# Down projection of a fused two-block kernel: one order of the k pairs for both halves, and the sums of weight blocks on GpSimd instead of VectorE

## The chip, the cores and the metric

One Trainium2 chip, one of its cores. Times are device microseconds (us) of one execution; the profile's durations of single instructions are in nanoseconds (ns) where marked. TensorE multiplies, VectorE and ScalarE prepare its operands, GpSimd does very little in this kernel, and SyncE's queue issues nearly all loads.

## The reference, cut to what matters

Two transformer blocks on a sequence of 256 tokens with a model width of 2048, all in float32. The change lies in the last stage of the second block, the down projection of the feed-forward part and the final norm:

```python
h = rmsnorm(x, g_ffn[l])
u = causal_dwconv(h @ w_up[l], ffn_conv_w[l]) + ffn_conv_b[l]
gate, val = jnp.split(u, 2, axis=-1)
x = x + (jax.nn.silu(gate) * val) @ w_down[l]
...
return rmsnorm(x, g_final)
```

`w_down` has 5632 rows (44 tiles of 128, taken as 22 k pairs of two tiles) and 2048 columns (four chunks of 512).

## The kernel before, in words

**How a product is made.** A float32 weight is split into a rounded part (hi) and the rest (lo). ScalarE copies a unit of 128x1024 weights from its stage into hi (line 676, `round_down`), VectorE subtracts hi from the stage to get lo (line 683, `rest_down`), and TensorE multiplies in three passes, activation-hi by weight-hi, activation-hi by weight-lo and activation-lo by weight-hi (lines 1245 to 1247). TensorE waits for `lo_ready` of each unit; ScalarE may round unit j only when TensorE has used unit j - 6, since hi and lo are rings of six slots (`DOWN_RING`). In the feed-forward stage ahead of it the same work is done at lines 346 and 351, with rings of four.

**Units of the down projection.** There are 116 units (`down_units`, line 131). A *row unit* is one k pair in one chunk of 512 columns: 2 k tiles x 2 token tiles x 3 passes = 12 matmuls of 512 columns. Its weights come through a ring of four stages. K pairs 7 to 21 are done in this way. K pairs 0 to 6 are done for two chunks at once by seven block products in place of eight (Strassen's scheme in Winograd's form): four units, here called s0 to s3, and 7 x 3 = 21 matmuls. Each uses up 6, 3, 6 and 6 of them. Their weights come into `pair_stage`, which holds two pairs. s0 and s1 are blocks as loaded; s2 and s3 need four sums of blocks, each 128x512, made in place in `pair_stage` after lo of s1 is done: two sums, then a signal (`sums_ready`) for which ScalarE's rounding of s2 waits, then two more sums and a signal for which the rounding of s3 waits. Before the change VectorE makes them, inside `rest_down` (lines 688 to 692). The activations' sums for these pairs are made earlier, in the feed-forward loop.

**The order.** The 2048 columns are done in two halves (chunks 0 and 1, then 2 and 3). `DOWN_PAIRS` (line 127) gives each half's order: a list of k pairs becomes row units, first all for the lower chunk, then all for the upper one; a bare number is one seven-product pair. In the first half the last list is `[20, 21]`, so the last seven-product pair is followed by four row units; in the second half it is `[18, 19, 20, 21]`, followed by eight. Every engine runs through the 116 units in this order: at step j ScalarE and VectorE prepare unit j + 5 (`prepared_at`, line 158; a little differently for the first steps) and do what else is due:

- steps 0 to 2: the last convolution, gate and activation of the feed-forward loop (`ffn_sums`, `ffn_conv`, `ffn_act`), on VectorE between its rests of units 3, 4 and 5;
- one and two steps after the last seven-product pair of a half (`SEVEN_END`): `add_sevens`, eight sums on VectorE that put the seven products into x;
- at the last row unit of a chunk (`DOWN_END`): `add_to_x` (line 454), which frees the chunk's two accumulator banks. Two pairs of banks take turns, so the first row unit of chunk 2 waits for `add_to_x` of chunk 0;
- two steps later `apply_gain` (line 2126): x of the chunk times the final gain, two products of 128x512. It waits for the squares of the chunk (line 530, ScalarE).

SyncE's queue issues the loads in the order of lines 773 to 779. A row load waits until lo of the unit four row units earlier is done; a pair's load waits until lo of s3 of the pair before the last is done. The first two pair loads wait until TensorE has finished the feed-forward stage, as `pair_stage` shares memory with that stage's operands. GpSimd's queue ends with the load of the final gain (line 872), after the last activation.

At the end, the last four row units are multiplied for token tile 0 first and then for tile 1 (lines 1289 to 1301). VectorE then finishes each tile: the last sum (line 2177), a reciprocal square root of 12 small steps, and two scalings; ScalarE scales the first half of the row (line 1611) and SyncE stores.

Of the kernel before, what the change touches and what calls it, by code (L numbers as in the profile page):

```python
# [33 lines left out]
LAYERS = 2  # L34
# [89 lines left out]
OUT_PAIRS = [0, 1, 2, 6, 7, 3, 4, 5]  # L124

SEVEN = 7
DOWN_PAIRS = [[[7, 8], 0, [9, 10], 1, [11, 12], 2, [13, 14], 3, [15, 16], 4, [17, 18], 5, [19], 6, [20, 21]],
              [[7, 8], 0, [9, 10], 1, [11, 12], 2, [13, 14], 3, [15], 4, [16], 5, [17], 6, [18, 19, 20, 21]]]


def down_units():

    units = []
    for chunk, items in enumerate(DOWN_PAIRS):
        for item in items:
            if isinstance(item, list):
                units += [("rows", k, 2 * chunk + half) for half in range(2) for k in item]
            else:
                units += [(f"seven{part}", item, chunk) for part in range(4)]
    return units  # L140


DOWN = down_units()
U_DOWN = len(DOWN)
DOWN_END = [max(j for j, unit in enumerate(DOWN) if unit[0] == "rows" and unit[2] == c) for c in range(4)]
SEVEN_END = [max(j for j, unit in enumerate(DOWN) if unit[0] == "seven3" and unit[2] == chunk) for chunk in range(2)]
DOWN_TAIL = U_DOWN - 4
DOWN_ROWS = [j for j, unit in enumerate(DOWN) if unit[0] == "rows"]
SEVEN_FIRST = [j for j, unit in enumerate(DOWN) if unit[0] == "seven0"]
# [3 lines left out]
def sevens_until(j):  # L153

    return sum(first <= j for first in SEVEN_FIRST)


def prepared_at(u):

    ahead = {0: [3], 1: [4], 2: [5], 3: [6, 7], 4: [8, 9]}.get(u, [u + 5])  # L160
    return [j for j in ahead if j < U_DOWN]
# [40 lines left out]
def build(nc, dram, out):  # L202
# [12 lines left out]
    with ctx:  # L215
        def sb(name, shape, dt=F32, stack=ctx):
            return stack.enter_context(nc.sbuf_tensor("sb_" + name, shape, dt))

        def sem(name):
            return ctx.enter_context(nc.semaphore(name))  # L220
# [9 lines left out]
        pair_stage = sb("pair_stage", [P, 2, 2, UNIT], F32, down)  # L230
# [29 lines left out]
        lo_ready = sem("lo_ready")  # L260
# [11 lines left out]
        mix_loaded, gfin_loaded, stored = sem("mix_loaded"), sem("gfin_loaded"), sem("stored")  # L272
# [12 lines left out]
        roped, pool_step = sem("roped"), sem("pool_step")  # L285
# [19 lines left out]
        sums_ready, first_copied, seven_free = sem("sums_ready"), sem("first_copied"), sem("seven_free")  # L305
# [148 lines left out]
        def add_to_x(dve, base, j, pair, c):  # L454

            multiplied(dve, base, j)
            for t in range(T):
                cols = x[:, t, c * 512:(c + 1) * 512]
                ins = dve.tensor_tensor(cols, acc[:, 2 * pair + t, :], cols, ALU.add)
            ins.then_inc(acc_free[pair], 1)  # L460
# [163 lines left out]
        U4 = U3 + N_FFN * U_FFN  # L624
# [23 lines left out]
        def down_parts(j):  # L648

            kind = DOWN[j][0]  # L650
            hi, lo = down_slot(j)
            if kind == "rows":
                return stage[:, DOWN_ROWS.index(j) % RING, :], hi, lo
            pair = pair_stage[:, (sevens_until(j) - 1) % 2, :, :]
            by_part = lambda ap: ap.rearrange("p (k n) -> p k n", n=512)
            if kind == "seven0":
                return pair[:, 0, :], hi, lo
            if kind == "seven1":
                return pair[:, 1, 512:UNIT], hi[:, 0:512], lo[:, 0:512]
            return pair[:, :, 0:512] if kind == "seven2" else pair[:, :, 512:UNIT], by_part(hi), by_part(lo)  # L660
# [14 lines left out]
            src, hi, _ = down_parts(j)  # L675
            act.activation(hi, src, ACT.Copy).then_inc(hi_ready, 1)

        def rest_down(step, dve, j):


            dve.wait_ge(hi_ready, U4 + (j + 1))
            src, hi, lo = down_parts(j)
            dve.tensor_tensor(lo, src, hi.bitcast(F32), ALU.subtract).then_inc(lo_ready, 1)
            if DOWN[j][0] == "seven1":
                pair = pair_stage[:, (sevens_until(j) - 1) % 2, :, :]
                b11, b22, b12, b21 = pair[:, 0, 0:512], pair[:, 0, 512:UNIT], pair[:, 1, 0:512], pair[:, 1, 512:UNIT]
                dve.wait_ge(lo_ready, U4 + (j + 1))
                step(dve.tensor_tensor(b11, b11, b12, ALU.add))
                dve.tensor_tensor(b12, b12, b22, ALU.add).then_inc(sums_ready, 1)
                dve.wait_ge(sums_ready, 2 * sevens_until(j) - 1)  # L690
                step(dve.tensor_tensor(b22, b11, b22, ALU.add))
                dve.tensor_tensor(b21, b22, b21, ALU.add).then_inc(sums_ready, 1)

        with nc.Block() as block:

# [93 lines left out]
            def _(pool):  # L789
# [29 lines left out]
                with pool.Fori(0, LAYERS) as layer:  # L819

                    pairs = layer * (C_LAYER // 2) + C_MEM // 2
                    step = Steps(pool, pool_step, layer * 19)
# [47 lines left out]

                pool.wait_ge(act_ready, N_FFN)
                pool.dma_start(gfin[:, :], dram["g_final_2"].partition_broadcast(P)).then_inc(gfin_loaded, 16)


            @block.tensor
# [740 lines left out]
            def _(dve):  # L1616
                step = Steps(dve, dve_step)
# [83 lines left out]
                with dve.Fori(0, LAYERS) as layer:  # L1701
# [6 lines left out]
                    step = Steps(dve, dve_step, layer * DVE_STEPS_LAYER + steps_before)  # L1708
# [103 lines left out]
                    for u in range(32):  # L1812
# [9 lines left out]
                        if u in (7, 15):  # L1822
                            j = u // 8
                            evacuate_scaled(dve, base, 48 + u, j, 512, lambda t: qb[:, t, j * RANK:(j + 1) * RANK], rstd)
                        if u in C_TURN:
                            j, t, use = C_TURN[u]
# [27 lines left out]
                step = Steps(dve, dve_step, steps_before + LAYERS * DVE_STEPS_LAYER)  # L1854
# [128 lines left out]
                for u in range(U_MIX):  # L1983
                    rest_unit(dve, U2, u + LEAD)
                    n, i = u // 4, u % 4
# [47 lines left out]
                def ffn_sums(turn_, back, half):  # L2033


                    tiles = half * FT - 2 * back
                    cols = bass.ds(turn_ * 2 + tiles, 2)
                    step(dve.tensor_scalar(taps[:, :, half, :], par_ffn[:, :, cols], 1.0, None, ALU.mult))
                    both_halves(half3, sum3, half, turn_ * 2 + (14 + half + 1 - 2 * back))
                    evacuated(dve, turn_ + (PAIRS3 - back), half)  # L2040
                    dve.tensor_tensor(sum3, sum3, again(rbc3[:, :], 2), ALU.mult).then_inc(sum_ready, 1)

                def ffn_conv(turn_, back, half, done=None):

                    y = value if half else gate
                    dve.wait_ge(tap2_done, turn_ * 2 + (half + 1 - 2 * back))
                    for d in (1, 2):
                        for k in range(2):
                            last = dve.scalar_tensor_tensor(out=y[:, k, d:SEQ], in0=sum3[:, k, 0:SEQ - d],  # L2049
                                                            scalar=taps[:, 2 - d, half, k:k + 1], in1=y[:, k, d:SEQ],  # L2050
                                                            op0=ALU.mult, op1=ALU.add)
                            if k == 1 and d == 1:
                                step(last)
                            elif k == 1:
                                if done is None:
                                    step(last)
                                else:
                                    last.then_inc(done, 1)
# [67 lines left out]
                def apply_gain(c):  # L2126

                    cols = slice(c * 512, (c + 1) * 512)
                    dve.wait_ge(x_squared, SQ_PRO * (3 + LAYERS) + 2 * (c + 1))
                    for t in range(T):  # L2130
                        ins = dve.tensor_tensor(x[:, t, cols], x[:, t, cols], gfin[:, cols], ALU.mult)
                    ins.then_inc(gain_applied, 1)
# [18 lines left out]

                for j in range(U_DOWN):
                    for ahead in prepared_at(j):
                        rest_down(step, dve, ahead)
                    if j == 0:
                        ffn_sums(N_FFN, 1, 1)
                    if j == 1:
                        ffn_conv(N_FFN, 1, 1)
                    if j == 2:
                        ffn_act(N_FFN, 1)  # L2160
                    if j - 1 in SEVEN_END:
                        add_sevens(SEVEN_END.index(j - 1), False)
                    if j - 2 in SEVEN_END:
                        add_sevens(SEVEN_END.index(j - 2), True)
                    if j in DOWN_END[:3]:
                        c = DOWN_END.index(j)
                        add_to_x(dve, U4, j, c % 2, c)
                    if j - 2 in DOWN_END[:3]:
                        if j - 2 == DOWN_END[0]:
                            dve.wait_ge(gfin_loaded, 16)  # L2170
                        apply_gain(DOWN_END.index(j - 2))

                dve.wait_ge(gain_applied, 3)
                third, last = slice(2 * 512, 3 * 512), slice(3 * 512, D)
# [33 lines left out]
```

## Time and profile before

| what | value |
|---|---|
| median of 3 runs | 1967.97 us (1967.76 to 1968.46) |
| the profiled execution's own time | 1967.66 us |
| its span in the trace | 1965.8 us |
| TensorE busy | 1939.5 us, 99% of the span |
| VectorE busy | 1373.9 us, 70% |
| ScalarE busy | 1049.5 us, 53% |
| GpSimd busy | 47.1 us, 2%, 74 instructions |
| start of the down projection in the trace | 1712.57 us |
| granted TensorE clock, mean | 0.996 |

The granted clock is 1.00 at full speed (2.4 GHz) and 0.50 at half speed (1.2 GHz). A matmul's printed duration (some 390 ns) is longer than the spacing of two matmuls, as they are pipelined; the spacing is what counts. A row such as "x2 | 2.35" in a timeline is two instructions joined. What an engine waited for stands in brackets or behind the last bar.

### The profile page before, as it was taken

Reading aid. Unit: us, or ns where it says so; the run is one execution under the profiler, and the core shown is the slowest. Engines: PE = TensorE matmul, PEld = TensorE weight load, DVE = VectorE, ACT = ScalarE, POOL = GpSimd, SP = SyncE. Lnnn points to the kernel's source line nnn. Section 1 sums busy time; section 2 is a strip of 40 time slices with the busy share of each in tenths; the row PEclk is TensorE's granted clock in tenths of the full one; section 3 lists DMA queues with packets and bytes.
Section 4 is the critical chain, followed back from the end, with each engine's and each line's share of the span. In section 5 each row is a group of like instructions: output and inputs, shape, how many; then the busy total and the mean of one; then the engine's idle time right before and its main releaser. Section 6 shows DMA issues by size and latency. Waiting matters only on the chain.

```text
span 1965.8 us, 28874 instructions
## 1 busy us (share of the span) xinstructions
PE 1939.5 (99%) x9826; PEld 1640.8 (83%) x9826; DVE 1373.9 (70%) x1948; ACT 1049.5 (53%) x1533; POOL 47.1 (2%) x74
## 2 busy tenths in 40 slices
PE   8999999999999999999999999999999999989997
PEld 7788888888888888888888888888888888878786
DVE  6655675656655675655767766888888777777877
ACT  5533576664433576664544444555555555454554
POOL 1000030000000020000100000000000000000000
PEclk9999999999999999999999999999999999999999
DMA  8666445545566545545665445556656556566563
GB/s 301 198 193 192 144 156 155 157 152 189 184 195 192 146 155 174 159 151 186 212 191 187 157 166 178 186 178 194 197 186 191 188 186 192 169 231 209 173 199 123
DMA packets 246727, 357.31 MB, mean 182 GB/s; under 512 B 15302, under 2 KB 136480, under 8 KB 246108
## 3 DMA queue, kind: packets, MB, share of 16 engines
q1 hardware_dynamic: 245004, 349.35, 56.3%
q0 software_dynamic: 1616, 6.61, 1.0%
q8 instruction: 58, 0.95, 0.2%
q14 instruction: 49, 0.40, 0.1%
HBM read 352.75 MB, written 3.16 MB: 181 GB/s over the span
## 4 chain that ended last, share of the span: by engine, by line
PE 93%; DVE 3%; DMA 2%; ACT 1%; issue 1%; SPq 0%; DVEq 0%; ACTq 0%
PE acc L411 21%; PE acc L388 15%; PE acc L390 15%; PE acc L389 15%; PE acc L404 11%; PE acc L1245 2%; PE acc L1246 2%; PE acc L1247 2%; PE aux L468 2%; PE aux L961 1%; PE aux L1245 1%; PE aux L1246 1%; PE aux L1247 1%; DVE sb_w_lo L351 1%; PE aux L979 1%
## 5 line engine op out<-in xcount | busy, mean ns | idle before, releaser
L351 DVE TENSOR_TENSOR sb_w_lo<-sb_stage,sb_w_hi 128x1024 fp32r<-128x1024 f32 x567 | 694.4, 1229 | 383.3 <-ACT sb_w_hi L346 376.2
L346 ACT ACTIVATE sb_w_hi<-sb_stage 128x1024 fp32r<-128x1024 f32 x567 | 598.3, 1058 | 491.8 <-PE acc L390 238.3
L411 PE MATMUL acc<-sb_xT,sb_w_hi 128*128 128x512 f32 x1856 | 445.7, 391 | 0.0
L411 PEld LDWEIGHTS acc<-sb_xT,sb_w_hi 128*128 128x128 f32 x1856 | 340.8, 188 | 65.8
L388 PE MATMUL acc<-sb_w_hi,sb_xT 128*128 128x512 f32 x768 | 306.2, 399 | 0.3 <-issue 0.3
L390 PE MATMUL acc<-sb_w_hi,sb_xT 128*128 128x512 f32 x768 | 299.5, 390 | 0.0
L389 PE MATMUL acc<-sb_w_lo,sb_xT 128*128 128x512 f32 x768 | 299.3, 390 | 0.0
L404 PEld LDWEIGHTS acc<-sb_xT,sb_w_lo 128*128 128x128 f32 x1856 | 238.7, 191 | 9.3
L404 PE MATMUL acc<-sb_xT,sb_w_lo 128*128 128x256 f32 x1856 | 243.0, 283 | 0.0
L388 PE MATMUL acc<-sb_w_hi,sb_mT 128*128 128x512 f32 x560 | 224.7, 401 | 1.3 <-issue 1.0
L390 PE MATMUL acc<-sb_w_hi,sb_mT 128*128 128x512 f32 x560 | 218.6, 390 | 0.0
L389 PE MATMUL acc<-sb_w_lo,sb_mT 128*128 128x512 f32 x560 | 218.4, 390 | 0.0
L390 PEld LDWEIGHTS acc<-sb_w_hi,sb_xT 128*128 128x128 f32 x768 | 144.2, 188 | 30.8
L388 PEld LDWEIGHTS acc<-sb_w_hi,sb_xT 128*128 128x128 f32 x768 | 144.3, 188 | 29.7 <-DVE sb_w_lo L351 0.7
L389 PEld LDWEIGHTS acc<-sb_w_lo,sb_xT 128*128 128x128 f32 x768 | 144.5, 188 | 27.8 <-issue 0.2
L388 PEld LDWEIGHTS acc<-sb_w_hi,sb_mT 128*128 128x128 f32 x560 | 105.2, 188 | 24.8 <-issue 1.6
L390 PEld LDWEIGHTS acc<-sb_w_hi,sb_mT 128*128 128x128 f32 x560 | 105.2, 188 | 22.9
L389 PEld LDWEIGHTS acc<-sb_w_lo,sb_mT 128*128 128x128 f32 x560 | 105.4, 188 | 20.0
L2049 DVE SCALAR_TENSOR_TENSOR sb_ffn_tmp<-sb_ffn_tmp,sb_taps 128x254 f32<-128x254 f32 (+1 forms) x176 | 77.3, 481 | 2.5
L1245 PE MATMUL acc<-sb_w_hi,sb_act_T 128*128 128x512 f32 x185 | 72.5, 392 | 0.0
L1246 PE MATMUL acc<-sb_w_lo,sb_act_T 128*128 128x512 f32 x185 | 72.3, 391 | 0.0
L1247 PE MATMUL acc<-sb_w_hi,sb_act_T 128*128 128x512 f32 x185 | 72.2, 390 | 0.0
(334 smaller groups left out, 1938.4 us busy)
## 6 DMA issues: line engine op xcount, KB each, us to landing
sb_stage<-w_in SPq DMA_DIRECT2D x248, 512.0 KB, 3.9
sb_stage<-w_up SPq DMA_DIRECT2D x176, 512.0 KB, 3.6
sb_stage<-w_out SPq DMA_DIRECT2D x96, 512.0 KB, 3.6
sb_stage<-w_down SPq DMA_DIRECT2D x60, 512.0 KB, 7.7
sb_pair_stage<-w_down SPq DMA_DIRECT2D x28, 512.0 KB, 7.5
sb_stage<-w_kv SPq DMA_DIRECT2D x16, 512.0 KB, 6.7
sb_stage<-w_ukv SPq DMA_DIRECT2D x16, 512.0 KB, 3.5
sb_stage<-w_uq SPq DMA_DIRECT2D x12, 512.0 KB, 3.5
```

Of the source, the lines that this page charges most:

```text
L346: act.activation(w_hi[:, j % RING, 0:size], stage[:, j % RING, 0:size], ACT.Copy).then_inc(hi_ready, 1)
L351: dve.tensor_tensor(w_lo[:, j % RING, 0:size], stage[:, j % RING, 0:size], w_hi[:, j % RING, 0:size].bitcast(F32), ALU.subtract).then_inc( ...
L388: pe.matmul(o, x_hi, hi[:, k, :], start=first and k == 0, stop=False)
L389: pe.matmul(o, x_hi, lo[:, k, :], start=False, stop=False)
L390: mm = pe.matmul(o, x_lo, hi[:, k, :], start=False, stop=last and k == nk - 1)
L404: mm = pe.matmul(acc[:, 2 * pair + c, 0:SEQ], lo[:, k, c * P:(c + 1) * P], xT[:, k0 + k, 0, :], start=False, stop=False)
L411: mm = pe.matmul(acc[:, 2 * pair + c, :], hi[:, k, c * P:(c + 1) * P], both, start=first and k == 0, stop=last and k == 3)
L468: mm = pe.transpose(aux[:, bank, i * P:(i + 1) * P], src(i), ident[:, :])
L1245: pe.matmul(o, a(0), hi, start=start, stop=False)
L1246: pe.matmul(o, a(0), lo, start=False, stop=False)
L1247: return pe.matmul(o, a(1), hi, start=False, stop=stop)
L2049: last = dve.scalar_tensor_tensor(out=y[:, k, d:SEQ], in0=sum3[:, k, 0:SEQ - d], scalar=taps[:, 2 - d, half, k:k + 1], in1=y[:, k, d:SEQ], ...
```

## The change

`DOWN_PAIRS` gets one order for both halves. GpSimd, which is otherwise done by then, makes the four sums of each of the 14 seven-product pairs, with the same waits and signals; VectorE no longer has them. The gains of chunks 0 and 1, which were applied early in the second half, are now both applied at step 110 (`SEVEN_END[1]` is 107), between the rest of unit 115 and `add_to_x` of chunk 2. That of chunk 2 stays at step 113.

```diff
-DOWN_PAIRS = [[[7, 8], 0, [9, 10], 1, [11, 12], 2, [13, 14], 3, [15, 16], 4, [17, 18], 5, [19], 6, [20, 21]],
-              [[7, 8], 0, [9, 10], 1, [11, 12], 2, [13, 14], 3, [15], 4, [16], 5, [17], 6, [18, 19, 20, 21]]]
+DOWN_PAIRS = 2 * [[[7, 8, 9], 0, [10, 11], 1, [12, 13], 2, [14], 3, [15], 4, [16], 5, [17], 6, [18, 19, 20, 21]]]
...
-        def rest_down(step, dve, j):
+        def rest_down(dve, j):
...
             dve.tensor_tensor(lo, src, hi.bitcast(F32), ALU.subtract).then_inc(lo_ready, 1)
-            if DOWN[j][0] == "seven1":
-                pair = pair_stage[:, (sevens_until(j) - 1) % 2, :, :]
+
+        def seven_sums(step, pool):
+
+            for n, first in enumerate(SEVEN_FIRST):
+                j, pair = first + 1, pair_stage[:, n % 2, :, :]
                 b11, b22, b12, b21 = pair[:, 0, 0:512], pair[:, 0, 512:UNIT], pair[:, 1, 0:512], pair[:, 1, 512:UNIT]
-                dve.wait_ge(lo_ready, U4 + (j + 1))
-                step(dve.tensor_tensor(b11, b11, b12, ALU.add))
-                dve.tensor_tensor(b12, b12, b22, ALU.add).then_inc(sums_ready, 1)
-                dve.wait_ge(sums_ready, 2 * sevens_until(j) - 1)
-                step(dve.tensor_tensor(b22, b11, b22, ALU.add))
-                dve.tensor_tensor(b21, b22, b21, ALU.add).then_inc(sums_ready, 1)
+                pool.wait_ge(lo_ready, U4 + (j + 1))
+                step(pool.tensor_tensor(b11, b11, b12, ALU.add))
+                pool.tensor_tensor(b12, b12, b22, ALU.add).then_inc(sums_ready, 1)
+                pool.wait_ge(sums_ready, 2 * n + 1)
+                step(pool.tensor_tensor(b22, b11, b22, ALU.add))
+                pool.tensor_tensor(b21, b22, b21, ALU.add).then_inc(sums_ready, 1)
...
                 pool.dma_start(gfin[:, :], dram["g_final_2"].partition_broadcast(P)).then_inc(gfin_loaded, 16)
+                seven_sums(Steps(pool, pool_step, LAYERS * 19), pool)
...
-                    if j - 2 in DOWN_END[:3]:
-                        if j - 2 == DOWN_END[0]:
-                            dve.wait_ge(gfin_loaded, 16)
-                        apply_gain(DOWN_END.index(j - 2))
+                    if j - 3 == SEVEN_END[1]:
+                        dve.wait_ge(gfin_loaded, 16)
+                        apply_gain(0)
+                        apply_gain(1)
+                    if j - 2 == DOWN_END[2]:
+                        apply_gain(2)
```

The units in order, with r for a row unit and S for the four units s0 to s3 of a pair:

```
before, chunks 0 and 1:  4r S 4r S 4r S 4r S 4r S 4r S 2r S 4r
before, chunks 2 and 3:  4r S 4r S 4r S 4r S 2r S 2r S 2r S 8r
after, either half:      6r S 4r S 4r S 2r S 2r S 2r S 2r S 8r
```

## Rows read from the trace of the kernel before

**Rows 1.** Waits of TensorE from 1700 us on: line, releaser, us, times, longest.
```profile
PE aux L1245 <- DVE sb_w_lo L683: 4.9, 1, 4.9
PE acc L1245 <- DVE sb_x L459: 2.4, 1, 2.4
PE acc L1245 <- DVE sb_down_lo L683: 0.5, 1, 0.5
```
**Rows 2.** Windows of 1 us: busy by engine, then PEclk, DMA share, GB/s.
```profile
1730.00:1731.00 1.00, 0.00 (x0) 0.00 (x0) 1.00 (x2) 1.00 (x2) 0.55 (x1) 0.72 0.00 0
1737.00:1738.00 1.00, 1.00 (x5) 0.81 (x4) 1.00 (x1) 0.50 (x1) 0.00 (x0) 0.87 0.69 156
...
1839.00:1840.00 1.00, 1.00 (x4) 0.86 (x5) 0.94 (x1) 0.97 (x3) 0.00 (x0) 0.83 0.06 23
1843.00:1844.00 1.00, 1.00 (x5) 0.75 (x4) 1.00 (x3) 0.10 (x1) 0.00 (x0) 0.96 0.03 10
```
**Rows 3.** Timeline of TensorE, eight matmuls before the middle wait: start, us.
```profile
1834.22 0.39 PE L1245 MATMUL acc<-sb_w_hi,sb_act_T 128*128 128x512 f32 x1
...
1836.03 0.39 PE L1247 MATMUL acc<-sb_w_hi,sb_act_T 128*128 128x512 f32 x1
```
**Rows 4.** Groups by line of the down projection: count, busy us, mean ns.
```profile
L683 DVE TENSOR_TENSOR sb_w_lo<-sb_stage,sb_w_hi 128x1024 fp32r<-128x1024 f32 x38 | 45.7, 1222 | 18.3 <-ACT sb_w_hi L676 17.4
L676 ACT ACTIVATE sb_w_hi<-sb_stage 128x1024 fp32r<-128x1024 f32 x38 | 39.5, 1056 | 24.3 <-PE acc L1247 23.7 <-DMA sb_stage<-w_down 0.6
...
L689 DVE TENSOR_TENSOR sb_pair_stage<-sb_pair_stage 128x512 f32<-128x512 f32 x13 | 9.0, 692 | 0.4
```
**Rows 5.** Timeline of VectorE: two rests back to back.
```profile
1732.34 2.35 DVE L683 TENSOR_TENSOR sb_w_lo<-sb_stage,sb_w_hi 128x1024 fp32r<-128x1024 f32 x2
```
**Rows 6.** Timeline of GpSimd in layer 1: start us, us, shapes.
```profile
286.65 0.73 POOL L848 TENSOR_TENSOR sb_kz<-sb_qb,sb_rope 128x256 f32<-128x256 f32 x1
...
288.27 1.30 POOL L843 TENSOR_TENSOR sb_kz<-sb_qb,sb_rope 128x512 f32<-128x512 f32 x1
289.65 0.73 POOL L846 TENSOR_TENSOR sb_kz<-sb_qb,sb_rope 128x256 f32<-128x256 f32 x1
290.46 1.60 POOL L847 TENSOR_TENSOR sb_kz<-sb_kz 128x256 f32<-128x256 f32 x1
```
**Rows 7.** Line L843 in all: GpSimd, 128x512, ns min/median/max.
```profile
L843 POOL TENSOR_TENSOR sb_kz<-sb_qb,sb_rope x4: 1301/1427/1553, 281.7 to 734.0; 128x512 f32<-128x512 f32 x4
```
**Rows 8.** Timeline of VectorE beside rows 6.
```profile
289.79 1.68 DVE L351 TENSOR_TENSOR sb_w_lo<-sb_stage,sb_w_hi 128x1024 fp32r<-128x1024 f32 x1 [0.19 <-ACT sb_w_hi L346]
```
**Rows 9.** Timeline: ScalarE hands over to GpSimd's first sum.
```profile
275.07 0.52 ACT L1385 ACTIVATE sb_kz<-aux,sb_rstd 128x64 f32<-128x64 f32 x2
...
275.85 0.45 POOL L830 TENSOR_TENSOR sb_kz<-sb_kz,sb_rope 128x128 f32<-128x128 f32 x1 [209.79 <-ACT sb_kz L1385]
```
**Rows 10.** Line L830's second row: a library command of GpSimd's queue.
```profile
L830 POOLq MODIFY_POOL_CONFIG  x4: 7/11/11, 275.7 to 721.5; - x4
```
**Rows 11.** Chain that ended last, from the start of the down projection: start, us.
```profile
1713.18 7.51 DMA sb_pair_stage<-w_down
1720.71 1.07 ACT sb_down_hi L676
...
1731.34 0.80 PE aux L1245
```
**Rows 12.** Timeline of VectorE: rests of units 106 and 107.
```profile
1926.19 2.44 DVE L683 TENSOR_TENSOR sb_down_lo<-sb_pair_stage,sb_down_hi 128x1024 fp32r<-128x1024 f32 x2
```
**Rows 13.** The same chain near the end: TensorE ends unit 103, lo of 109.
```profile
1928.95 0.24 PE acc L1247
...
1930.37 1.24 DVE sb_w_lo L683
1931.62 5.25 DMA sb_stage<-w_down
```
**Rows 14.** Timeline of VectorE at the end: the gain of chunk 2.
```profile
1950.04 1.29 DVE L2131 TENSOR_TENSOR sb_x<-sb_x,sb_ffn_tmp 128x512 f32<-128x512 f32 x2 [1.55 <-ACT sb_junk L530]
```

More of the change, by code:

```diff
@@ L2153, in _ @@
                     for ahead in prepared_at(j):
-                        rest_down(step, dve, ahead)
+                        rest_down(dve, ahead)
                     if j == 0:
```

## The prediction

> **What bounds the kernel now.** I read the page first: TensorE is busy for 99% of the span, so time is won or lost where it waits or where its clock falls. In the down projection its waits come to three: 0.5 and 4.9 us for lo of the first seven-product pair, and 2.4 us for `add_to_x` of chunk 0 in the middle [rows 1]. The clock falls twice, to half speed: from some 1730.44 to 1737.3 (the 1-us windows at either edge show a mean of 0.72 and 0.87), of which TensorE worked 6.0 us and so lost 3.0, and from 1839.66 to 1843.07, which lost 1.7 [rows 2]. Elsewhere a matmul follows the last by 0.2267 us (8 of them in 1.81 us) [rows 3], so a row unit takes 12 x 0.2267 = 2.72 us, a seven-product pair 4.76, and two row units with a pair 10.2 us. That last figure is the clock that the other engines must keep up with in a short period ("2r S"). Durations are of the profiled execution, 1967.66 us, 0.3 below the median; I add the sum to the former.
>
> **Price of a sum on GpSimd.** VectorE's sum takes 0.69 us [rows 4], 0.72 with its own wait, so it is rid of 4 x 0.72 = 2.9 us per pair. GpSimd's nearest row is a product of 128x512: 1.30 us while VectorE had no instruction that reads twice from SBUF, up to 1.55 otherwise [rows 6, 7]; the next instruction starts 0.08 later. With 0.73 for 256 columns [rows 6] the slope gives the same 1.30. I take 1.38 us start to start, 5.5 us for four. The lower end is 1.2 (another pattern of operands), the upper 1.55. The Trainium skill ("GPSIMD Engine Reference", 3, Performance versus the Vector engine) puts GpSimd's two-input sum at 1.96 times VectorE's; from 0.69 that estimate is 1.36 us and would add 1.5 us to the sum below.
>
> **Beside VectorE.** GpSimd's 256 columns took 1.60 us in place of 0.73 when VectorE was in a rest (290.46 against 286.65) [rows 6], and the rest that began at 289.79 took 1.68 in place of 1.22, until just after GpSimd's instruction ended at 290.38 [rows 8]. So whoever comes second stands until the first is through. In each pair one rest, that of s2, meets the sums 3 and 4: it asks 1.1 us after sum 2, stands 0.15, and sum 4 then stands 0.7. Ends: 0 (no meeting) and 1.2 (sum 4 stands for the whole rest).
>
> **Handing over.** ScalarE's line 1385 ended at 275.59, GpSimd began at 275.85 [rows 9]: 0.25 us into GpSimd. Back to ScalarE no row shows; between 0.05, as among the other engines, and 0.25. I take 0.05, as nothing in the rows makes the receiver slow.
>
> **The short periods.** ScalarE goes through the units in order, so its round of s3 stands in front of the next pair's. The loop, from the round of s3 to that of the next s3: round 1.06, five rests on VectorE (s3 1.22, two rows and s0 at 1.13 back to back [rows 5], s1 0.69) make 6.4 us; then 0.25, 5.5 of sums, 0.05: 12.2, and 12.9 with the meeting. Before, the sums in this place took 2.9 on VectorE, the loop 9.3, under 10.2, so it was hidden. Now it exceeds TensorE's 10.2 by 2.7 us (2.0 without meeting). The first short period of a half has slack: counted from TensorE's start on pair 2, ScalarE may round pair 3's s0 at 1.36; lo of s1 is done at 4.3, the sums at 10.1 (10.8), lo of s3 at 12.4 (13.1); TensorE wants it at 10.2 + 3.4 = 13.6. Slack 0.5 (1.2). The order now has four short periods in each half (before one and three): three full losses behind the slack, 3 x 2.7 - 0.5 = 7.6, twice: **+15.2 us**. Long periods ("4r S", 15.6 us) hide a loop of 12.9 + 2.1.
>
> **The head.** Six row units stand ahead of the first pair, not four: TensorE has 5.4 us more to do before it wants s2. Lo of s2 was done at 1731.3, by a chain from the pair's landing at 1720.7 [rows 11]. The new chain starts from the loads of units 4 and 5, which SyncE issues right behind the pair's, so at about the same time. It has two rests more (2.4) and no sums on VectorE (-2.9), but 0.25 and two of GpSimd's (2.8) and a round (1.06) that the other work had hidden: 3.7 us later. The wait of 5.4 becomes 3.7, and 0.9 more before s3, whose sums meet the rest. **-0.8 us**; the fall of the clock stays, as the wait is still long. Ends -3.8 (no fall) and +2 (the two row loads slower).
>
> **The middle.** After S the first half now has eight row units. `add_sevens` and `add_to_x` of chunk 0 run under the last four, and chunk 1's banks are wanted only after three more of chunk 2. The wait of 2.4 and the fall of the clock behind it go: **-4.1 us**, none late next. VectorE's eight sums and the two of `add_to_x` (some 7 us) lie under 10.9 us of matmuls.
>
> **The end.** There VectorE sets the pace. Two gains move in ahead of `add_to_x` of chunk 2: 4 x 0.65 [rows 14] = +2.6; where they stood before (steps 57 and 59) taking them away wins nothing beyond what the middle has. Further: before, the rest of unit 107 ended at 1928.6 [rows 12], 3.7 ahead of TensorE's need (1928.95 + 15 x 0.2267 = 1932.35). Now TensorE waits for it, and the rests of 108 and 109, the load that 109 frees (5.25), and all that follows come later against TensorE: lo of 109 was done 0.75 before TensorE began 107 [rows 13], now 2.3 after. **+3.0**, ending in some 2 us of waiting before unit 115, no extra cost as VectorE is later still. Sum **+5.6 us**; ends 2.6 and 7.
>
> **Loads.** The bytes are the same, and a row load now waits for rests that are later, but is wanted later as well. SyncE's queue holds a row load behind a pair's in places; ends 0 and +2. The gain's load stays ahead of the sums in GpSimd's queue: 0.6 us, hidden before s1 is done.
>
> **Sum**: 15.2 - 0.8 - 4.1 + 5.6 = +15.9; 1967.66 + 15.9 = **1983.6 us**, slower by 0.8%.
>
> **The rivals.**
> 1. *Sums and rests overlap freely.* Loop 12.2: losses 2 x (3 x 2.0 - 1.2) = 9.6, sum +10.3, 1978 us; with sums of 1.2 us the loop is 11.5, the losses some 4 and the end less late, 1972. Against it: rows 6 and 8. Chance 0.2.
> 2. *Sum 4 always stands behind a whole rest, and handing back costs 0.2.* Loop 13.6, excess 3.4: 2 x (3 x 3.4) = 20.4 in place of 15.2, 1989 us; with sums of 1.55, four times 0.17 more in each of six periods, 1993. For it: the meeting is a matter of 0.1 us, sum 4 asks just as the rest starts. Beside it stands a rule of the Trainium skill ("SBUF — State Buffer", Who interferes with whom): the first holds the shared ports for its whole instruction. Chance 0.2.
> 3. *GpSimd keeps up, and the kernel gets faster.* The place is the short period. The point is a sum of (10.2 - 6.4 - 0.3) / 4 = 0.87 us with all meetings. Below it the losses vanish, the end costs only 2.6, the head gains 1.5 more: -0.8 - 1.5 - 4.1 + 2.6 = -3.8, and 3.0 more if the clock doesn't fall: 1961 to 1964 us. For it: VectorE is rid of 40 us and the middle wait is sure to go. Against it: 1.30 us in rows 6 and 7. Chance 0.07.
> 4. *A code load before GpSimd's first sum.* The Trainium skill ("GPSIMD Engine Reference", 2.1, Instruction dispatch) tells of a first call after a load of code that costs about 6 us and has no instruction in the profile. Line 830 shows the command [rows 10], and its sum began 0.25 us after its releaser [rows 9], so here the load was hidden or absent. In the head nothing would hide it: 6 us more before s2, 1990 us. Chance 0.03, the page's estimate alone giving the size.
>
> **How the numbers follow.** The forecast has 0.45: its own range is 1979 to 1988. Rivals 1 to 4 have 0.2, 0.2, 0.07 and 0.03; 0.05 is left for a sum near zero (sums of about 1.0 us, part of the losses cancelling the middle). The range that leaves out 0.2: 1972 to 1994. A measurement here tells 0.2% (3.9 us) from no change. Faster 0.08, same 0.07, slower 0.85.
>
> **What would show it.** VectorE's busy time falls by about 39 us, GpSimd's rises to about 120 to 135 us. TensorE's waits: one of some 4 us for lo of s2 and one under 1 us for s3 in the head; none for `add_to_x`; in each half about three periods with waits of 2 to 3 us for lo of s2 or s3 in pairs 4, 5 and 6, little in pair 3 and none in pairs 1 and 2; about 2 us before unit 115. ScalarE's waits for its round of s2 and s3 are ended by GpSimd. From TensorE's start on unit 107 to the end takes some 6 us more than before. GpSimd's sums take 1.30 us, the fourth of a pair about 2.0. Wrong would be: pairs 4 to 6 without waits (a shorter sum or more lead), or waits in long periods too (a longer loop).

## The result, and the profile after

| what | before | after |
|---|---|---|
| median | 1967.87 us (4 runs, 1964.56 to 1968.46) | 1986.79 us (4 runs, 1983.98 to 1987.40) |
| ratio, 95% interval | | 1.0096 [1.0083, 1.0109] |
| the profiled execution | 1967.66 us, span 1965.8 | 1983.98 us, span 1982.1 |

The change makes the kernel slower by 1.0%. The two spans differ by 16.3 us; the medians by 18.9, since the profiled execution after is the quickest of its four. The parts below are read from the two spans.

The page of the changed kernel, its part 1 (busy us with share and count):

```profile
PE 1944.8 (98%) x9826; PEld 1640.6 (83%) x9826; DVE 1335.3 (67%) x1892; ACT 1045.4 (53%) x1533; POOL 131.3 (7%) x130
```

VectorE has 38.6 us and 56 instructions less, GpSimd 84.2 us and 56 instructions more. TensorE does the same matmuls; its busy share hardly moves (98%, before 99%), as the losses are some 1% of the span. The waits show them. TensorE's waits from 1700 us on (line, releaser, us in total, times, longest), where before stood those of [rows 1]:

```profile
PE aux L1249 <- DVE sb_w_lo L682: 8.6, 5, 3.4
PE aux L1249 <- DVE sb_down_lo L682: 4.3, 3, 1.8
PE acc L1302 <- DVE sb_w_lo L682: 1.6, 1, 1.6
PE acc L1249 <- DVE sb_down_lo L682: 1.1, 1, 1.1
```

The wait for `add_to_x` in the middle is gone. In its place stand eight waits for lo of s2 or s3 (the lines with `aux`) and one for the last unit. Where they lie is seen in the timeline of TensorE (start, us; in brackets the wait). The first three are the head: unit 4, then s2 and s3 of pair 0. Then come s3 of pairs 3 to 6 of the first half, and the last is unit 115:

```profile
1724.52 0.50 PE L1249 MATMUL acc<-sb_down_hi,sb_act_T 128*128 128x512 f32 x1 [1.09 <-DVE sb_down_lo L682]
1736.16 0.50 PE L1249 MATMUL aux<-sb_w_hi,sb_seven_T 128*128 128x512 f32 x1 [3.35 <-DVE sb_w_lo L682]
1739.64 0.79 PE L1249 MATMUL aux<-sb_w_hi,sb_seven_T 128*128 128x512 f32 x1 [0.90 <-DVE sb_w_lo L682]
...
1783.02 0.39 PE L1249 MATMUL aux<-sb_w_hi,sb_seven_T 128*128 128x512 f32 x1
...
1795.40 0.50 PE L1249 MATMUL aux<-sb_w_hi,sb_seven_T 128*128 128x512 f32 x1 [1.85 <-DVE sb_w_lo L682]
...
1808.09 0.64 PE L1249 MATMUL aux<-sb_w_hi,sb_seven_T 128*128 128x512 f32 x1 [1.83 <-DVE sb_w_lo L682]
...
1820.79 0.50 PE L1249 MATMUL aux<-sb_w_hi,sb_seven_T 128*128 128x512 f32 x1 [0.62 <-DVE sb_w_lo L682]
...
1961.25 0.50 PE L1302 MATMUL acc<-sb_w_hi,sb_act_T 128*128 128x512 f32 x1 [1.55 <-DVE sb_w_lo L682]
```

Pair 3 has no wait, pairs 4 and 5 have the large ones, and pair 6 a small one, since the clock had fallen behind pair 5 and TensorE was later. The second half repeats this with 1.85, 1.83 and 0.60 us for pairs 4 to 6.

TensorE names VectorE as what it waited for, and VectorE had been standing for ScalarE. What ScalarE in turn had stood for is told by its own waits:

```profile
ACT sb_w_hi L675 <- POOL sb_pair_stage L692: 38.4, 8, 7.1
ACT sb_down_hi L675 <- POOL sb_pair_stage L692: 27.4, 6, 5.1
ACT sb_w_hi L675 <- POOL sb_pair_stage L695: 20.3, 8, 2.5
ACT sb_down_hi L675 <- POOL sb_pair_stage L695: 15.2, 6, 2.5
```

All 28 rounds of s2 and s3 wait for GpSimd, 101 us together. The groups of GpSimd in the down projection (count, busy us, mean ns) show four sums that are the same work, and one that takes longer:

```profile
L695 POOL TENSOR_TENSOR sb_pair_stage<-sb_pair_stage 128x512 f32<-128x512 f32 x14 | 30.1, 2151 | 1.1
L694 POOL TENSOR_TENSOR sb_pair_stage<-sb_pair_stage 128x512 f32<-128x512 f32 x14 | 18.1, 1294 | 1.1
L691 POOL TENSOR_TENSOR sb_pair_stage<-sb_pair_stage 128x512 f32<-128x512 f32 x14 | 18.0, 1287 | 123.0 <-DVE sb_down_lo L682 69.7 <-DVE sb_w_lo L682 53.3
L692 POOL TENSOR_TENSOR sb_pair_stage<-sb_pair_stage 128x512 f32<-128x512 f32 x14 | 18.0, 1287 | 1.1
```

How the fourth comes by its 2.15 us is seen beside VectorE's rest of s2, in the timelines of both (start, us):

```profile
1803.22 1.33 DVE L682 TENSOR_TENSOR sb_w_lo<-sb_pair_stage,sb_w_hi 128x1024 fp32r<-128x1024 f32 x1 [3.86 <-ACT sb_w_hi L675]
```

```profile
1802.16 1.30 POOL L694 TENSOR_TENSOR sb_pair_stage<-sb_pair_stage 128x512 f32<-128x512 f32 x1
1803.54 2.15 POOL L695 TENSOR_TENSOR sb_pair_stage<-sb_pair_stage 128x512 f32<-128x512 f32 x1
```

The rest begins under the third sum and takes 0.11 us more than its 1.22; the fourth sum begins 0.32 us behind the rest and takes 0.86 more than its neighbours.

The loop itself stands in the chain of waits of the changed kernel (start, us). From 1786.74 to 1820.8 no matmul is in it:

```profile
1786.74 1.30 POOL sb_pair_stage L691
...
1788.11 1.30 POOL sb_pair_stage L692
...
1789.47 1.30 POOL sb_pair_stage L694
1790.78 0.07 issue
1790.85 2.17 POOL sb_pair_stage L695
1793.01 0.02 issue
1793.03 1.07 ACT sb_w_hi L675
1794.10 0.02 issue
1794.12 3.50 DVE sb_w_lo L682 x3
1797.62 1.75 DVE sb_down_lo L682 x2
1799.37 0.07 issue
1799.43 1.29 POOL sb_pair_stage L691
```

Four sums and their gaps 6.29, round 1.09, five rests 5.25, 0.06: 12.69 us from the first sum of a pair to the first of the next (1786.74 to 1799.43). TensorE needs 10.2 us for the same units. What that costs is counted in the windows of 41 us that hold three such loops (us, then busy by engine with counts, granted clock, DMA share, GB/s), first half and second half:

```profile
1783.00:1824.00 41.00, 36.65 (x150) 28.60 (x149) 22.60 (x21) 18.64 (x21) 18.07 (x12) 0.96 0.54 174
...
1905.00:1946.00 41.00, 36.67 (x150) 28.62 (x150) 22.61 (x21) 18.90 (x21) 18.05 (x12) 0.96 0.45 146
```

150 matmuls in each, where 41 / 0.2267 = 181 fit: 31 x 0.2267 = 7.0 us lost in each window. Counted without the windows' edges: from the first matmul of pair 3 to that of the second row unit behind pair 6 there are 168 matmuls, 38.1 us at full speed. They took 45.4 us in each half (1779.62 to 1825.05 and 1901.89 to 1947.30), so 7.3 us were lost. The granted clock is 0.96 in both windows, so it fell there as well. That comes out of TensorE's waits and costs nothing beyond them, as the loop holds no matmul: three loops are 3 x (12.69 - 10.2) = 7.5 us longer than TensorE's work, less a slack of 0.2.

### The profile page after: what moved, and what is told of

Its sections match the earlier page's. It is cut to its first block, busy times and chain, and to the rows that moved or that the text cites. A ratio compares the mean times of both kernels' runs of the same rounds, so it can differ in the third digit from the quotient of the medians.

```text
span 1982.1 us, 28874 instructions
## 1 busy us (share of the span) xinstructions
PE 1944.8 (98%) x9826; PEld 1640.6 (83%) x9826; DVE 1335.3 (67%) x1892; ACT 1045.4 (53%) x1533; POOL 131.3 (7%) x130
## 4 chain that ended last, share of the span: by engine, by line
PE 88%; DVE 4%; POOL 3%; DMA 2%; ACT 1%; issue 1%; POOLq 0%; SPq 0%; DVEq 0%; ACTq 0%
PE acc L410 21%; PE acc L387 15%; PE acc L389 15%; PE acc L388 15%; PE acc L403 11%; PE aux L467 2%; DVE sb_w_lo L682 2%; PE acc L1249 2%; PE acc L1250 2%; PE acc L1251 2%; POOL sb_pair_stage L695 1%; DVE sb_down_lo L682 1%; DMA sb_stage<-w_kv 1%; DMA sb_stage<-w_down 1%; PE aux L965 1%
## 5 line engine op out<-in xcount | busy, mean ns | idle before, releaser
L1249 PE MATMUL acc<-sb_w_hi,sb_act_T 128*128 128x512 f32 x192 | 75.9, 395 | 0.0
L1251 PE MATMUL acc<-sb_w_hi,sb_act_T 128*128 128x512 f32 x192 | 75.5, 393 | 0.0
```

Of the source, the lines that this page charges most:

```text
L1249: pe.matmul(o, a(0), hi, start=start, stop=False)
L1251: return pe.matmul(o, a(1), hi, start=False, stop=stop)
```

## The experiments

Each kernel was timed against the kernel before in the same rounds (the latter at 1966.99 us in the first four, 1967.08 in the others).

**The order alone.** The kernel before with the new `DOWN_PAIRS` only.

```diff
-DOWN_PAIRS = [[[7, 8], 0, [9, 10], 1, [11, 12], 2, [13, 14], 3, [15, 16], 4, [17, 18], 5, [19], 6, [20, 21]],
-              [[7, 8], 0, [9, 10], 1, [11, 12], 2, [13, 14], 3, [15], 4, [16], 5, [17], 6, [18, 19, 20, 21]]]
+DOWN_PAIRS = 2 * [[[7, 8, 9], 0, [10, 11], 1, [12, 13], 2, [14], 3, [15], 4, [16], 5, [17], 6, [18, 19, 20, 21]]]
```

> The kernel before with the new order of k pairs alone: VectorE keeps the sums, the gains stay two steps after each chunk. The loop theory: the loss of the change comes from the loop ScalarE-VectorE-GpSimd in the short periods and its lateness at the end, so the order alone must be faster than before: the middle gives 4.1 us, the head 3 to 4 us (5.4 us more of matmuls ahead of the first pair, no sums on GpSimd), and the short periods cost nothing, as the loop with sums on VectorE is 9.3 us against TensorE's 10.2. Expected 1959 to 1961 us, against 1967.9 before, no wait of TensorE in pairs 3 to 6. The order theory (four short periods in each half are too tight for the loads and for VectorE by themselves): 1970 us or more, with waits in pairs 4 to 6.

Measured: 1960.20 us (5 runs, 1958.87 to 1961.73), ratio 0.9963 [0.995, 0.9977]. All of TensorE's waits from 1700 us on:

```profile
PE aux L1244 <- DVE sb_w_lo L682: 2.3, 1, 2.3
PE acc L1244 <- DVE sb_down_lo L682: 0.9, 1, 0.9
```

Both are in the head; four short periods in each half are no burden while VectorE makes the sums. The order theory falls: this part of the change is a gain of 6.8 us.

**The sums on GpSimd alone.** The changed kernel with the old `DOWN_PAIRS` and the old places of the gains.

```diff
-DOWN_PAIRS = 2 * [[[7, 8, 9], 0, [10, 11], 1, [12, 13], 2, [14], 3, [15], 4, [16], 5, [17], 6, [18, 19, 20, 21]]]
+DOWN_PAIRS = [[[7, 8], 0, [9, 10], 1, [11, 12], 2, [13, 14], 3, [15, 16], 4, [17, 18], 5, [19], 6, [20, 21]],
+              [[7, 8], 0, [9, 10], 1, [11, 12], 2, [13, 14], 3, [15], 4, [16], 5, [17], 6, [18, 19, 20, 21]]]
...
-                    if j - 3 == SEVEN_END[1]:
...
+                    if j - 2 in DOWN_END[:3]:
...
```

> The kernel before with the sums on GpSimd alone: old order, old places of the gains. The loop theory: second half three short periods, two full losses of 2.5 us less some slack, 4.7 us; first half none; head +2 us (one more round and the fourth sum's meeting); middle +3 us, since lo of the last pair's s3 is late and add_sevens with it; end +3 us for the late rests. Sum about +13 us, 1981 us. The order theory, by which GpSimd's sums are hidden and the order costs: 1968 us or a little under.

Measured: 1983.16 us (5 runs, 1980.07 to 1984.52), ratio 1.0076 [1.0062, 1.009]. Its waits of TensorE from the middle on:

```profile
PE acc L1250 <- DVE sb_x L459: 5.9, 1, 5.9
PE aux L1250 <- DVE sb_down_lo L683: 2.4, 2, 1.8
PE acc L1303 <- DVE sb_w_lo L683: 1.6, 1, 1.6
```

The total is 2 us above what was expected. The spacing of TensorE's matmuls gives the parts: against the kernel before, the head cost 3.5 us more (2 expected; its wait for s2 is 6.7 us, and the fall of the clock is longer), the middle 4.0 (3 expected), the short periods of the second half 4.9 (4.7) and the end 3.1 (3). The middle's wait grew from 2.4 to 5.9, as expected: the late s3 of the last pair pushes the rests, the loads and `add_sevens` behind it.

The two parts of the change don't add up: -6.8 for the order and +16.2 for the sums would be +9.4, and together they gave +18.9. The traces show where they meet. The new order gives the sums on GpSimd eight short periods to spoil, not four: TensorE loses 14.7 us in them, against 4.9. It takes away the middle, which had grown to 8.3 us with the fall of the clock, and the end is 2.4 us longer with the gains' new place.

**The gains back in their old place.** The changed kernel with the four lines of `apply_gain` as before.

```diff
-                    if j - 3 == SEVEN_END[1]:
-                        dve.wait_ge(gfin_loaded, 16)
-                        apply_gain(0)
-                        apply_gain(1)
...
+                    if j - 2 in DOWN_END[:3]:
+                        if j - 2 == DOWN_END[0]:
+                            dve.wait_ge(gfin_loaded, 16)
+                        apply_gain(DOWN_END.index(j - 2))
```

> The changed kernel with the gains of chunks 0 and 1 back two steps after their chunks. If four products of 0.65 us stand on the path that sets the end, this is 2.5 us faster than the changed kernel (1984.2 against 1986.8) and the waits of TensorE stay as they are. If the gains' place was made to keep VectorE free for the pairs after the middle, some wait shows up there and the time stays at 1986.8 or rises.

Measured: 1984.52 us (5 runs, 1983.68 to 1986.80), ratio 1.0088 [1.0074, 1.0102]. That is 2.3 us under the changed kernel's median, near the size expected, but the intervals of the two ratios overlap, and the two profiled executions stand the other way (1984.80 against 1983.98). So a gain is not shown.

The waits do not stay as they were. The largest of the short periods are the same (1.84 us), but pair 3 of each half now waits 0.82 us, and the first pair of the second half, a long period, has a wait that the changed kernel has not. It stands behind VectorE's products with the gain of chunk 1, which come between its rests of s0 and s1 (TensorE, then VectorE):

```profile
1865.01 0.50 PE L1249 MATMUL aux<-sb_w_hi,sb_seven_T 128*128 128x512 f32 x1 [0.74 <-DVE sb_w_lo L682]
```

```profile
1854.37 1.29 DVE L2135 TENSOR_TENSOR sb_x<-sb_x,sb_ffn_tmp 128x512 f32<-128x512 f32 x2
1855.57 0.69 DVE L682 TENSOR_TENSOR sb_down_lo<-sb_pair_stage,sb_down_hi 128x512 fp32r<-128x512 f32 x1
```

GpSimd's first sum of this pair begins at 1856.34, in the changed kernel at 1853.21, 3.1 us later, where TensorE reaches the pair only 0.3 later (1860.71 and 1860.41). From the start of this pair to the row unit behind pair 6 TensorE loses 9.7 us in place of 7.3; from that unit to the end it is 1.8 us quicker (35.8 for 37.6). So both readings of the expectation are right in part: the place near the end costs there what it saves behind the middle, once the sums are on GpSimd.

**GpSimd for the pairs in long periods only.** In the changed kernel the sums of pairs 3 to 6 of each half went back to VectorE.

```diff
...
             for n, first in enumerate(SEVEN_FIRST):
+                if n % SEVEN >= 3:
+                    continue
...
+                        if DOWN[ahead][0] == "seven1" and (sevens_until(ahead) - 1) % SEVEN >= 3:
+                            dve_sums(step, dve, ahead)
```

> The changed kernel, but with the sums of pairs 3 to 6 of each half (those behind two row units) back on VectorE; GpSimd makes them for pairs 0 to 2 only, in long periods. The loop theory: the long periods hide GpSimd's sums, so the losses of 13 us in the short periods and the 3 us of lateness at the end go; left are the head's -0.8, the middle's -4.1 and the gains' +2.6: 1966 us. The rival theory that each meeting on the shared port costs wherever it happens: 6 of 14 pairs keep their share, about 1974 to 1976 us.

Measured: 1965.84 us (11 runs, 1964.97 to 1968.12), ratio 0.9995 [0.9986, 1.0004]. The same two windows as above:

```profile
1783.00:1824.00 41.00, 41.00 (x182) 33.95 (x182) 35.52 (x38) 23.73 (x25) 0.00 (x0) 1.00 0.72 231
1905.00:1946.00 41.00, 41.00 (x182) 33.97 (x181) 35.82 (x39) 20.10 (x21) 0.00 (x0) 1.00 0.45 143
```

182 matmuls in place of 150, no wait. Six pairs keep their sums on GpSimd, with the meeting in each, and from the third row unit behind pair 0 on TensorE loses nothing up to its last matmul: five of the six pairs are free. The medians of this kernel and the changed one differ by 21 us, the two traces by 16.2. In the traces the changed kernel loses 14.7 us in the short periods and 3.4 in what follows from the last of them; 1.8 us go the other way, as it began the stage 1.3 us earlier and lost 0.5 less in the head.

The sixth, the first pair of all, is not free. All of TensorE's waits lie there:

```profile
PE aux L1263 <- DVE sb_w_lo L682: 5.2, 2, 3.4
PE acc L1263 <- DVE sb_down_lo L682: 1.1, 1, 1.1
```

That is 6.3 us against 3.2 in the order alone. Counted by the spacing of the matmuls, with the fall of the clock in it, the head lost 9.9 us against 5.9. This and the gains' place, which costs 2.4 us at the end of the trace, are what keeps this kernel 5.6 us behind the order alone (1960.20). Where GpSimd's sums are hidden they cost nothing, but they win nothing either.

**No meeting.** The changed kernel, with ScalarE's round of s2 waiting for the fourth sum.

```diff
             if kind == "seven2":
-                act.wait_ge(sums_ready, 2 * n + 1)
+                act.wait_ge(sums_ready, 2 * n + 2)
```

> The changed kernel, but ScalarE rounds s2 only after the fourth sum, not after the second. No rest of VectorE then runs beside a sum. The port theory: the fourth sum takes 2.15 us because it stands while VectorE's rest of s2 reads; now it must take 1.29 like the others in all 14 pairs, and the rest of s2 1.22 in place of 1.33. The loop is 4 x 1.37 + 1.11 + six rests 6.4 = 13.0 us against 12.7, six times, and the head waits some 1 to 2 us more: 1989 us, a little slower than the changed kernel in spite of the faster sum. The pattern theory (the fourth sum is slow by its own operands): it stays at 2.15, and the loop is 13.8 us: 1994 us or more.

Measured: 1989.87 us (4 runs, 1989.35 to 1990.69), ratio 1.0115 [1.01, 1.0131]. The group of the fourth sum, and two neighbouring first sums in the chain:

```profile
L695 POOL TENSOR_TENSOR sb_pair_stage<-sb_pair_stage 128x512 f32<-128x512 f32 x14 | 18.0, 1287 | 1.1
```

```profile
1789.28 1.30 POOL sb_pair_stage L691
...
1802.24 1.29 POOL sb_pair_stage L691
```

The fourth sum takes 1287 ns when no rest of VectorE runs beside it, and 2151 when one does. That shows the cause of the 0.86 us. The loop is 12.96 us, as reckoned (13.0): the meeting bought an overlap worth a little more than it cost.

**Two sums each.** In the changed kernel the first two sums of every pair went back to VectorE.

```diff
...
-                pool.wait_ge(lo_ready, U4 + (j + 1))
-                step(pool.tensor_tensor(b11, b11, b12, ALU.add))
-                pool.tensor_tensor(b12, b12, b22, ALU.add).then_inc(sums_ready, 1)
                 pool.wait_ge(sums_ready, 2 * n + 1)
...
+                        if DOWN[ahead][0] == "seven1":
+                            dve_sums(step, dve, ahead)
```

> The changed kernel with the first two sums of each pair on VectorE, only the last two on GpSimd. The loop theory, from durations of the changed kernel's trace: rests 5.25, two sums 1.44, then on GpSimd 1.37 and 2.2, round 1.1: 11.4 us, 1.2 above TensorE's 10.2 in place of 2.5. With 1.9 us of slack in the first short period the losses are 2 x (3 x 1.2 - 1.9) = 3.6 in place of about 13, the head is 1.3 better, the end the same: 1970 to 1973 us. The rival, that what costs is any meeting of GpSimd and VectorE (each pair still has one, of the same length): no more than 2 to 3 us better than the changed kernel, 1984 us.

Measured: 1972.62 us (8 runs, 1970.74 to 1973.31), ratio 1.0027 [1.0016, 1.0038]. The timeline of GpSimd (start, us, in brackets the wait):

```profile
1797.01 1.30 POOL L700 TENSOR_TENSOR sb_pair_stage<-sb_pair_stage 128x512 f32<-128x512 f32 x1 [7.89 <-DVE sb_pair_stage L691]
1798.38 2.15 POOL L701 TENSOR_TENSOR sb_pair_stage<-sb_pair_stage 128x512 f32<-128x512 f32 x1
1808.42 1.31 POOL L700 TENSOR_TENSOR sb_pair_stage<-sb_pair_stage 128x512 f32<-128x512 f32 x1 [7.89 <-DVE sb_pair_stage L691]
```

The loop is 11.41 us, as worked out beforehand, with the same meeting in it. The excess over 10.2 falls from 2.5 to 1.2 us, and the median by 14 us. In the traces the short periods lost 4.4 us in place of 14.7 (the expectation's 2 x (3 x 1.2 - 1.9) is 3.4, not the 3.6 that it gives). Another 3.0 us lie in the head, where the waits are shorter and the clock did not fall. So the length of the loop decides, not the meeting.

**The middle alone.** The kernel before with the second half's old order in both halves.

```diff
-DOWN_PAIRS = [[[7, 8], 0, [9, 10], 1, [11, 12], 2, [13, 14], 3, [15, 16], 4, [17, 18], 5, [19], 6, [20, 21]],
+DOWN_PAIRS = [[[7, 8], 0, [9, 10], 1, [11, 12], 2, [13, 14], 3, [15], 4, [16], 5, [17], 6, [18, 19, 20, 21]],
               [[7, 8], 0, [9, 10], 1, [11, 12], 2, [13, 14], 3, [15], 4, [16], 5, [17], 6, [18, 19, 20, 21]]]
```

> The kernel before with the first half in the order that its second half had: only the middle changes (one more run of two row units, eight row units after the last pair). Sums on VectorE. If the middle is worth what the wait of 2.4 us and the fall of the clock behind it show, 4.1 us are won and the head stays: 1963 us, and TensorE has no wait for add_to_x.

Measured: 1962.85 us (11 runs, 1962.25 to 1963.97), ratio 0.9978 [0.9969, 0.9987]: 4.2 us won, for 4.1 reckoned. Its waits of TensorE are those of the head alone, 4.9 and 0.6 us.

**A version that beats both.** Sums on VectorE, eight row units ahead of the first pair. The kernel that ran has this in the first half alone, unlike what the expectation says: the second half keeps its old order, with four row units ahead and three short periods.

```diff
-DOWN_PAIRS = [[[7, 8], 0, [9, 10], 1, [11, 12], 2, [13, 14], 3, [15, 16], 4, [17, 18], 5, [19], 6, [20, 21]],
+DOWN_PAIRS = [[[7, 8, 9, 10], 0, [11, 12], 1, [13], 2, [14], 3, [15], 4, [16], 5, [17], 6, [18, 19, 20, 21]],
               [[7, 8], 0, [9, 10], 1, [11, 12], 2, [13, 14], 3, [15], 4, [16], 5, [17], 6, [18, 19, 20, 21]]]
```

> A version meant to beat both: sums on VectorE, each half begins with eight row units [7, 8, 9, 10] and goes on with [11, 12], [13], and so on, so that each half has five short periods. The wait for s2 in the head was 2.3 us with six row units and VectorE's sums; two more row units (5.4 us) cover it, and the fall of the clock behind it goes: another 3.5 to 5 us below the order alone, 1955 to 1957 us. The loop with sums on VectorE is 9.3 us, so a fifth short period costs nothing. If the short periods were at their limit by the loads, waits would show there and the time would be 1960 us or more.

Measured: 1956.76 us (5 runs, 1956.43 to 1957.08), ratio 0.9946 [0.9933, 0.996], 10.3 us under the kernel before and 30 under the changed one. The five short periods of the first half cost nothing. One wait is left, for unit 4 in the head, and the clock is at 1.00 in the head's window, where before it had the fall of [rows 2]:

```profile
PE acc L1245 <- DVE sb_down_lo L683: 1.7, 1, 1.7
```

```profile
1712.00:1742.00 30.00, 28.31 (x124) 22.64 (x123) 20.52 (x26) 11.93 (x14) 0.55 (x1) 1.00 0.75 246
```

## Why the prediction was right

It said 1983.6 us and slower by 0.8%; measured were 1986.8 and 1.0%. By its own steps, in the two profiled executions (losses are TensorE's time over 0.2267 us per matmul, from the starts in its timeline):

- **Price of a sum.** 1.38 us start to start was taken, 1.37 measured (1786.74 to 1788.11). The row of an unrelated product of the same size [rows 6] carried over to a sum in place.
- **Beside VectorE.** One meeting per pair with 0.7 us for sum 4 was taken; 0.86 measured, in all 14 pairs, and 0.1 for the rest. The run without the meeting shows the cause. The Trainium skill ("SBUF — State Buffer", Who interferes with whom) lets the second stand until the first is through. By that rule sum 4, which starts at 1803.54 with 1.01 us of the rest to go, would last 1.01 + 1.29 = 2.30 us, and the rest, which starts 0.24 before the end of sum 3, 1.22 + 0.24 = 1.46. They lasted 2.15 and 1.33, and the rest of [rows 8] took 1.68 where the rule makes it 0.59 + 1.22 = 1.81. So the rule gives the size, and each time 0.13 to 0.15 us too much; why, no run shows. What counts is how much of the other instruction is left when the second one asks, not its whole length.
- **Handing over.** 0.25 us was taken; the chain shows 0.07. The loop was put at 12.9 and measured 12.69, and this is the difference. (The 0.16 more of the meeting was made up where sum 4 hands on: 0.02 us, where a gap of 0.08 and 0.05 had been counted.) What the rest of the 0.25 was in [rows 9] no run here shows.
- **Short periods.** 7.6 us per half reckoned, as three full losses less a slack. Measured 7.3 in the first half and 7.2 in the second up to unit 107: three losses of 2.49, less 0.2. Pairs 1 to 3 had no waits; the small one is in pair 6, where the fall of the clock had taken its share.
- **The head.** -0.8 reckoned, +0.5 came, and this step is wrong. The waits of 3.35 and 0.90 us came as said (3.7 and 0.9). What failed is "at about the same time" for the loads of the two new row units: the load of unit 4 landed at 1722.15, the pair's had at 1720.7, and it cost a wait of 1.09. The head's waits sum to 5.3, as before (5.4), and the fall of the clock was longer. To the third row unit behind pair 0 the head lost 9.4 us (117 matmuls from 1712.39 to 1748.34), before 8.8 (93 from 1712.57 to 1742.42); the start was 0.2 earlier.
- **The middle.** -4.1 reckoned. Before, wait and fall of the clock lost 4.3; the wait is gone, and the run with the middle alone gave 4.2.
- **The end.** +5.6 reckoned. From TensorE's start on unit 107 (1943.04, behind a wait) to the end of the last scaling (1977.88) it is 34.8 us; before, 1932.42 and 1961.57: 29.2. The difference is 5.7. The wait before unit 115 was 1.55 for some 2.

The difference of the spans, 16.3 us, splits into 10.6 up to unit 107 and 5.7 behind it; the sum said 15.9. That it is so near is in part luck: the head came out 1.3 us worse than reckoned, the short periods 0.7 and the middle 0.2 better. The medians' further 2 to 3 us come with lower mean clocks (0.992 and 0.993 in the other three runs, 0.994 in the profiled one), so with more time at half speed. Some may lie ahead of the down projection: it began at 1712.39 in this trace and between 1713.07 and 1714.01 in those of the five other kernels with sums on GpSimd. Where the rest lay no trace shows.

Of the rivals, free overlap (1978) is refuted by the 2151 ns, the fourth sum behind a whole rest with a slow way back (1989) by the same number, which is 0.86 above a sum alone and not 1.2, and a handing back of 0.02 us, the faster kernel by the 1.29 us of a sum against the 0.87 that it needed. A code load before the first sum: GpSimd's first sum began at 1731.05, lo of s1 ended at 1730.96, and no gap of some 6 us stands before it.

## What to carry to other kernels

An engine that is 70% busy on average may still be the wrong one to relieve. What counts is the loop of waits that must fit into the bound engine's shortest period: here it went from 9.3 us (reckoned) to 12.7 (measured) with 10.2 to fit in, though VectorE was rid of 39 us of work and GpSimd stood idle for 93% of the span. Sum the loop over all engines, with each queue's order, before work is handed to a slower one. A helper belongs where the period is long and something lies ahead to hide it: five such pairs were free, and the first pair of the stage cost 4 us.

A schedule's gain and a placement's loss can sit in one change and hide each other: the order alone was worth 7 us, and with VectorE's sums it could be pushed to 10.

## What had not been expected

- The run with the gains in the old place has the same long wait in the head as the changed kernel (3.36 for 3.35 us), yet its clock did not fall there. Windows of 4 us, first of it, then of the changed kernel:

```profile
1740.00:1744.00 4.00, 3.59 (x16) 2.96 (x17) 4.00 (x5) 4.00 (x6) 0.00 (x0) 1.00 0.30 88
```

```profile
1740.00:1744.00 4.00, 4.00 (x11) 3.12 (x11) 4.00 (x4) 3.58 (x5) 0.00 (x0) 0.57 0.50 149
```

  16 matmuls against 11 in the same time: 1.1 us from the clock alone, and 1.7 over the whole head (7.8 us lost for 9.4). So a wait of some 3 us may or may not cost a fall, in executions of much the same program.
- Most of those 1.7 us came back. Where the clock had not fallen, TensorE came earlier to the short periods and waited 0.82 us for s3 of pair 3, where the changed kernel has no wait. By the end of the first half's pairs the two had lost 16.4 and 16.8 us. In these two traces the fall of the clock, ahead of a stretch whose pace another chain of work sets, was largely paid by the waits that it shortened.
- Taking the meeting on the port away made the kernel slower (12.96 for 12.69 us per loop), since a contended overlap still was an overlap.
